# Gate and up projections of a gated FFN as seven block products instead of eight, in a one-core encoder-layer kernel

## The reference

```
def swiglu(x, w_gate, w_up, w_down):
    return (jax.nn.silu(x @ w_gate) * (x @ w_up)) @ w_down
...
D_MODEL = 1024; SEQ = 512; D_FF = 2816
u = rmsnorm(h, ffn1_pre_norm[i])
h = h + 0.5 * rmsnorm(swiglu(u, ffn1_w_gate[i], ffn1_w_up[i], ffn1_w_down[i]), ffn1_post_norm[i])
```

## Time and profile before

| | |
|---|---|
| median of 3 runs | 1209.6 us (1209.51 to 1209.68) |
| span of the profiled execution | 1207.3 us |
| median less span | 2.3 us |
| PE busy | 1198.1 us, 99% |
| PE weight loads busy | 972.3 us, 81% |
| DVE busy | 642.7 us, 53% |
| ACT busy | 466.0 us, 39% |
| POOL busy | 110.2 us, 9% |
| instructions | 15098 |

### The profile page before, as it was taken

One profiled execution on the slowest core, in us unless ns is written; L12 is line 12 of the kernel. 1 busy time (PEld: TensorE's weight loads), 2 busy tenths in 40 slices (PEclk: granted clock), 3 DMA queues, 4 the chain that ended last, 5 costly groups with the idle time before them and its releaser, 6 DMA issues.

```text
span 1207.3 us, 15098 instructions
## 1 busy us (share of the span) xinstructions
PE 1198.1 (99%) x5564; PEld 972.3 (81%) x5564; DVE 642.7 (53%) x1019; ACT 466.0 (39%) x703; POOL 110.2 (9%) x95
## 2 busy tenths in 40 slices
PE   9999999999999999999999999999999999999998
PEld 8888888888888886567887888788888888888887
DVE  6644444462227797755567874674344444222584
ACT  6322333222125537566333623552223232121473
POOL 3000000000004100000012201210000000000254
PEclk9999999999999999999999999999999999999998
DMA  6333232322231341111522233332332323232211
GB/s 224 118 104 103 89 104 87 104 89 103 95 90 53 71 122 53 36 36 36 158 87 71 84 108 105 105 105 87 104 100 91 104 87 105 88 104 92 100 36 70
DMA packets 101840, 111.85 MB, mean 93 GB/s; under 512 B 15294, under 2 KB 91678, under 8 KB 101542
## 3 DMA queue, kind: packets, MB, share of 16 engines
q1 hardware_dynamic: 97542, 109.18, 29.0%
q10 hardware_dynamic: 4256, 2.12, 0.6%
HBM read 108.12 MB, written 3.16 MB: 92 GB/s over the span
## 4 chain that ended last, share of the span: by engine, by line
PE 92%; DVE 3%; ACT 2%; issue 1%; POOL 0%; ACTq 0%; DVEq 0%; POOLq 0%
PE bank L294 25%; PE bank L296 25%; PE bank L295 25%; PE bank L602 2%; PE bank L596 2%; PE bank L597 2%; PE bank L301 1%; PE bank L303 1%; PE bank L302 1%; PE bank L1062 1%; PE bank L436 1%; PE bank L1041 1%; DVE small L1343 1%; PE bank L1729 1%; PE bank L1172 1%
## 5 line engine op out<-in xcount | busy, mean ns | idle before, releaser
L324 DVE TENSOR_TENSOR w_lo<-w_raw,w_hi 128x1024 fp32r<-128x1024 f32 x193 | 242.5, 1262 | 352.5 <-ACT w_hi L317 350.8
L294 PE MATMUL bank<-v_hi,w_hi 128*128 128x512 f32 x904 | 356.8, 395 | 0.0
L296 PE MATMUL bank<-v_hi,w_lo 128*128 128x512 f32 x904 | 352.3, 390 | 0.0
L295 PE MATMUL bank<-v_lo,w_hi 128*128 128x512 f32 x904 | 351.9, 389 | 0.0
L317 ACT ACTIVATE w_hi<-w_raw 128x1024 fp32r<-128x1024 f32 x193 | 202.3, 1056 | 356.4 <-PE bank L296 352.5
L294 PEld LDWEIGHTS bank<-v_hi,w_hi 128*128 128x128 f32 x904 | 169.7, 188 | 38.2 <-issue 3.5
L296 PEld LDWEIGHTS bank<-v_hi,w_lo 128*128 128x128 f32 x904 | 169.7, 188 | 35.7
L295 PEld LDWEIGHTS bank<-v_lo,w_hi 128*128 128x128 f32 x904 | 169.9, 188 | 34.0
L294 PE MATMUL bank<-prod_hi,w_hi 128*128 (+1 forms) x352 | 137.1, 389 | 0.0
L296 PE MATMUL bank<-prod_hi,w_lo 128*128 (+1 forms) x352 | 136.9, 389 | 0.0
L295 PE MATMUL bank<-prod_lo,w_hi 128*128 (+1 forms) x352 | 136.9, 389 | 0.0
(11 more groups left out here) (274 smaller groups left out, 1342.2 us busy)
## 6 DMA issues: line engine op xcount, KB each, us to landing
w_raw<-in_ffn_w_up SPq DMA_DIRECT2D x44, 512.0 KB, 3.5
w_raw<-in_ffn_w_down SPq DMA_DIRECT2D x44, 512.0 KB, 3.4
w_raw<-in_ffn_w_gate SPq DMA_DIRECT2D x43, 512.0 KB, 3.6
w_raw<-in_w_in SPq DMA_DIRECT2D x32, 512.0 KB, 3.7
w_raw<-in_w_out SPq DMA_DIRECT2D x8, 512.0 KB, 3.3
w_raw<-in_ple_w_gate SPq DMA_DIRECT2D x8, 512.0 KB, 3.3
x_tm<-in_x SPq DMA_DIRECT2D x4, 512.0 KB, 6.6
Mb<-m_rows ACTq DMA_DIRECT2D x8, 256.0 KB, 5.0
```

Source lines behind the costliest of these rows:

```text
L294: nc.tensor.matmul(o, whi, a_hi, start=start, stop=False)
L295: nc.tensor.matmul(o, whi, a_lo, start=False, stop=False)
L296: return nc.tensor.matmul(o, wlo, a_hi, start=False, stop=stop)
L324: nc.vector.tensor_tensor(w_lo[:, s, :], w_raw[:, s, :], w_hi[:, s, :].bitcast(F32), ALU.subtract).then_inc(w_lo_done, 1)
```

## The change

Steps 0 and 1 keep the ordinary product (`LEADS = 2`). In the other nine steps of each FFN the gate and the up product (256 features x 1024 x 512 tokens each) are one "quad" each: the 256 output features, the 1024 input features and the 512 tokens are cut in halves, and seven products of 128 features x 512 x 256 tokens replace the eight, by Strassen's scheme in Winograd's form. A quad has 7 products of 12 matmuls with 256 tokens, so 84 in place of 48 with 512 tokens.

- The sums of token blocks (`T1` to `T4`) are made once in each FFN: GpSimd makes the unsplit input `vraw` from `h` beside the sums of squares, DVE the differences, ACT and DVE split them.
- The sums of weight blocks (`S1` to `S4`, 128x512 each) are made by GpSimd in each quad, four instructions, from the raw chunks in `w_raw` to `wsum` (one buffer). ACT and DVE split them in place of raw chunks: 3.5 chunks of 1024 a quad (`group_hi`, `group_lo`, g = 0 to 3), in place of 2 a quad before.
- Partial results are copied from PSUM by ACT (`r_copy_act`) and added to by DVE (`posts_dve`), four times a quad, in `scratch`.
- The gate is scaled and the product made with one instruction of 1024 columns each (`gate_scale_dve`, `prod_dve`), the silu also; the second multiplication by `r_b` falls away, and the norm behind the FFN takes an epsilon divided accordingly (`epsr`).
- The product is kept unsplit (`prod`) and split during the down product (`phi_act`, `plo_dve`), one tile for each chunk, in four slots of `T_hi` and `T_lo`.
- The loop stays on PE alone; DVE, ACT, SP and POOL are written out.

```diff
+        def block_pe(pe, i, q):
+            b = 4 - 4 * q
...
+            own.wait(pe, "post", 8 * i + (4 * q - 4 + POST0 - 8 * LEADS))
+            own.wait(pe, "lead_out", 4 + 4 * q)
+            weights(0)
+            product(0, 0, P, *v(0, 0), 0, 0, True)
+            weights(1)
+            product(1, 0, 2 * P, *v(1, 0), 1, 0, True)
+            weights(2)
+            own.wait(pe, "t_lo", T1 + 1)
+            product(2, 0, P, *T(T1), 2, 1, True)
+            weights(3)
+            own.wait(pe, "t_lo", T2 + 1)
+            own.wait(pe, "rcopy", 6 * i + (3 * q + 1 - 6 * LEADS))
+            product(3, 0, P, *T(T2), 0, 0, False)
+            own.wait(pe, "t_lo", T4 + 1)
+            product(1, P, 2 * P, *T(T4), 2, 0, False)
+            own.wait(pe, "t_lo", T3 + 1)
+            own.wait(pe, "rcopy", 6 * i + (3 * q + 2 - 6 * LEADS))
+            product(2, 4 * P, P, *T(T3), 0, 0, False)
+            product(3, 4 * P, P, *v(1, 1), 3, 0, True)
...
+        FREED = (1, 5, 6, 7)
+        def group_hi(act, qd, g):
...
+            if g < 2:
+                act.wait_ge(*raw_loaded(qd, g))
+            else:
+                own.wait(act, "s_sum", 4 * qd + 2 * g - 2)
...
+                own.wait(act, "mm", 7 * (qd - 1) + FREED[g])
...
+        def r_copy_act(act, qd, e):
+            if qd >= 2 and e == 0:
+                own.wait(act, "prod_ready", LEADS + qd // 2)
+            own.wait(act, "mm", 7 * qd + (1, 4, 6)[e])
...
             # ACT
+            for qd in range(QUADS):
+                r_copy_act(act, qd, 0)
+                group_hi(act, qd + 1, 0)
+                if qd % 2 == 1:
+                    silu_act(act, LEADS + qd // 2)
+                r_copy_act(act, qd, 1)
+                group_hi(act, qd + 1, 1)
+                r_copy_act(act, qd, 2)
+                group_hi(act, qd + 1, 2)
+                if qd == QUADS - 1:
+                    phi_act(act, 0)
+                group_hi(act, qd + 1, 3)
             # DVE
+            for qd in range(QUADS):
+                posts_dve(dve, qd, 0)
+                group_lo(dve, qd + 1, 0)
+                posts_dve(dve, qd, 1)
+                group_lo(dve, qd + 1, 1)
+                posts_dve(dve, qd, 2)
+                group_lo(dve, qd + 1, 2)
+                if qd == QUADS - 1:
+                    plo_dve(dve, 0)
+                posts_dve(dve, qd, 3)
+                group_lo(dve, qd + 1, 3)
+                if qd % 2 == 0:
+                    gate_scale_dve(dve, LEADS + qd // 2)
+                else:
+                    prod_dve(dve, LEADS + qd // 2)
...
+        def pool_prog(pool):
+            def keep_raw(m):
+                nc.gpsimd.tensor_tensor(vraw[:, m, :], h[:, m, :], pre(m).broadcast_to([P, S]), ALU.mult).then_inc(own["vraw_ready"], 1)
+            h_squares_pool(pool, n, keep_raw)
+            for qd in range(QUADS):
...
+                if qd >= 1:
+                    own.wait(pool, "s_lo", 4 * (qd - 1) + 3)
+                nc.gpsimd.tensor_tensor(S1, A21, A22, ALU.add).then_inc(own["s_sum"], 1)
+                nc.gpsimd.tensor_tensor(S3, A11, A21, ALU.subtract).then_inc(own["s_sum"], 1)
+                if qd >= 1:
+                    own.wait(pool, "s_lo", 4 * (qd - 1) + 4)
+                own.wait(pool, "s_sum", 4 * qd + 1)
+                nc.gpsimd.tensor_tensor(S2, S1, A11, ALU.subtract).then_inc(own["s_sum"], 1)
+                own.wait(pool, "s_sum", 4 * qd + 3)
+                nc.gpsimd.tensor_tensor(S4, A12, S2, ALU.subtract).then_inc(own["s_sum"], 1)
```

More of the change, by code:

```diff
@@ L577, in h_squares_pool @@
                 nc.gpsimd.tensor_tensor(sqacc[:], sqacc[:], scratch[:, m % 4, :], ALU.add).then_inc(b["h_acc"], 1)
+            if beside is not None and m < 5:
+                beside(m)
+        if beside is not None:
+            for m in range(5, KD):
+                beside(m)
     def lead_pe(pe, n, N, x_tiles=None):
@@ L676, in sp_prog @@
                 after_lead(sp)
-            with sp.Fori(1, NI) as i:
+            for i in range(1, NI):
                 for j in range(4):
-                    sp.wait_ge(w_lo_done, 4 * i + (N + j - RING + 1))
-                    sp_load(sp, i, j)
[L682 to L688, removed]
@@ new lines, in block_pe, with product, weights, v @@
+        def block_pe(pe, i, q):
+            b = 4 - 4 * q
+            def product(g, off, step, a_hi, a_lo, bank, half, start):
+                s = (N + g) % RING
+                for kk in range(4):
+                    c = off + step * kk
+                    whi, wlo = w_hi[:, s, c:c + P], w_lo[:, s, c:c + P]
+                    o = B[b + bank][:, 256 * half:256 * half + 256]
+                    nc.tensor.matmul(o, whi, a_hi(kk), start=(start and kk == 0), stop=False, skip_group_check=True)
+                    nc.tensor.matmul(o, whi, a_lo(kk), start=False, stop=False, skip_group_check=True)
+                    last = nc.tensor.matmul(o, wlo, a_hi(kk), start=False, stop=(kk == 3), skip_group_check=True)
+                last.then_inc(own["mm"], 1)
+            def weights(g):
+                own.wait(pe, "s_lo", 8 * i + (4 * q + g + 1 - 8 * LEADS))
+            def v(half, t):
+                return [lambda kk, v_=v_: v_[:, 4 * half + kk, 256 * t:256 * t + 256] for v_ in (v_hi, v_lo)]
+            def T(x):
+                return [lambda kk, t_=t_: t_[:, x, kk, :] for t_ in (T_hi, T_lo)]
+            own.wait(pe, "post", 8 * i + (4 * q - 4 + POST0 - 8 * LEADS))
[17 more added lines that the diff above has]
+            product(3, 4 * P, P, *v(1, 1), 3, 0, True)
@@ L709, in down @@
+            with pe.Fori(LEADS, NI) as i:
+                for q in range(2):
+                    block_pe(pe, i, q)
             def down(k, j, first=False):
                 pe.wait_ge(w_lo_done, k + (DN + 1))
-                ph = prod_hi[:, k, :] if isinstance(k, int) else prod_hi[:, bass.ds(k, 1), :].rearrange("p a s -> p (a s)")
-                pl = prod_lo[:, k, :] if isinstance(k, int) else prod_lo[:, bass.ds(k, 1), :].rearrange("p a s -> p (a s)")
+                own.wait(pe, "plo", k + 1)
@@ L713, in down @@
                 for m in range(KD):
[L714 to L718, removed]
+                    if first and m in (0, 4):
+                        own.wait(pe, "post", POST0 + 4 * (QUADS - 1 + m // 4))
+                    last = three(B[YBANK[m]][:], wv(DN + j, m * P, (m + 1) * P), split_slot(T_hi, j), split_slot(T_lo, j),
+                                 first, False)
@@ L754, in ups_dve @@
[L754 to L766, removed]
@@ new lines, in phi_act, with plo_dve @@
+        def phi_act(act, k):
+            own.wait(act, "prod_ready", k // 2 + 1)
+            if k < 4:
+                own.wait(act, "mm", 7 * (QUADS - 1) + 3 + k // 2)
+            else:
+                act.wait_ge(w_used, DN + k - 3)
+            nc.scalar.activation(split_slot(T_hi, k), prod[:, k, :], ACT.Copy).then_inc(own["phi"], 1)
+        def plo_dve(dve, k):
+            own.wait(dve, "phi", k + 1)
+            nc.vector.tensor_tensor(split_slot(T_lo, k), prod[:, k, :], split_slot(T_hi, k).bitcast(F32),
+                                    ALU.subtract).then_inc(own["plo"], 1)
@@ L770, in dve_prog @@
+        def dve_prog(dve, between=None, late=None, arena_free=None):
+            if n == 0:
+                dve.sem_inc(own["post"], POST0)
             lead_dve(dve, n, N)
-            gates_dve(dve, 0, True)
+            gate_scale_dve(dve, 0)
+            T_raw_dve(dve, T1)
             lo_upto(dve, N + 6)
[L773 to L780, removed]
+            T_raw_dve(dve, T2)
+            prod_dve(dve, 0)
+            T_raw_dve(dve, T4)
+            T_raw_dve(dve, T3)
+            lo_upto(dve, N + 7)
+            for x in range(4):
+                T_lo_dve(dve, x)
+            group_lo(dve, 0, 0)
+            group_lo(dve, 0, 1)
+            gate_scale_dve(dve, 1)
+            group_lo(dve, 0, 2)
+            group_lo(dve, 0, 3)
+            prod_dve(dve, 1)
+            if arena_free is not None:
+                arena_free(dve)
+            for qd in range(QUADS):
[11 more added lines that the diff above has]
+                    gate_scale_dve(dve, LEADS + qd // 2)
+                else:
+                    prod_dve(dve, LEADS + qd // 2)
+            for k in range(1, 4):
+                plo_dve(dve, k)
```

309 lines of the change are left out of this document (224 added, 85 removed).

## The result

The changed kernel takes 1252.2 us (median of 4 runs, 1248.4 to 1254.6), beside 1209.6 us before (1209.5 to 1210.3): a ratio of 1.0347, 95% interval 1.0328 to 1.0366. It is slower, as forecast, but by 42.6 us in place of 22.6, and the median lies 2 us above the predicted range.

A forecast was written before the change was run, and what follows sets the result against it. PE's matmul stream bounds the kernel before. Per FFN the quads, with DVE and POOL taking turns, add 8.1 us, the down product's turn 2.7, `vraw` 0.5; twice that is +22.6: 1232 us against 1209.6, range 1196 to 1250.

The forecast's parts named there:

- The mechanism: In the quads, DVE instructions with two SBUF inputs and POOL TENSOR_TENSORs exclude each other and, both queued, take turns.
- The chain from A: From A, the end of an odd quad's sixth product, to the next quad's fourth product, starting at A+8.4, undisturbed A+5.5.
- even P4: Fourth product of even quads: PE starts it 2.9 us late, released by ACT's `scratch` copy.
- the rival of 1196 us: DVE keeps the turn, so S3 falls behind `prod` and `gate_scale`; a pair takes 20.9 us; chance 0.15.
- The mean of `group_lo`: Sign in DVE's splits of the quads: mean well above 1.26 us, 1.5 or more.
- three instructions on one resource: In a quad, 4.2 + 1.2 us of DVE and 4.2 to 5.2 of POOL: about 10 of 9.66 us.
- The narrow matmul: PE's matmul of 256 columns in the quads: 0.115 us, between 0.111 and 0.120; a quad 9.66 us.
- odd P6: Sixth product of odd quads: PE starts it 1.2 us late.
- the clock: Rival: the clock falls in PE's 32 waits, up to +54 us, 1286; chance 0.12 together with slow narrow matmul or loop.
- The nine steps: The nine loop steps of each FFN before the change, which the quads replace: 196.2 us.
- The turns: Start of each down product: its first chunk waits for `plo` of tile 0, +2.7 us an FFN.
- The start of the quads: The 8 `vraw` instructions between and behind the squares mostly hide: 0.5 us an FFN, 0 to 1.5.

The follow-up runs named there:

- e5: The change with one wait number altered: POOL's S1 waits for DVE's split of g=3 in place of g=2; 1203.2 us, ratio 0.9949.
- e7: The change plus second buffer for partial results, S1 behind g=3 and earlier first split of the down product; 1183.3 us, in a second run 1183.2.
- e9: As e7, but the last three `vraw` instructions of each boundary wait until DVE has the second root; 1183.5 us, ratio 0.9786.
- e4: The change plus 18 unused matmuls of 256 columns ahead of the fourth product of each even quad; 1244.6 us, ratio 1.0276.
- e3: The change without the third matmul of each weight (low weights by high tokens) in the quads; 1239.9 us, ratio 1.0252.

## Where the prediction held, and the step that failed

**The mechanism held, with its times.** The chain from A ended at A+8.2 (A+8.4 predicted with 1.29 us for a sum). Late at even P4: 2.47 us, 2.9 predicted; the first matmul after a wait adds 0.11. DVE and POOL took turns: the second sum of a quad, S3, waited for one DVE instruction and then ran in all 36 quads (2.26 to 2.29 us each); that DVE would keep the turn, the rival of 1196 us, was not seen. The mean of `group_lo` was 1697 ns (1.5 us or more predicted), `prod` 2173 (2.2). The Trainium skill (GPSIMD Engine Reference, section 1, Specifications) names this contention, without a figure. The runs give one: a wait for one instruction of the other engine.

**Not quite as said.** I put the loss to three instructions on one resource, "about 10 of 9.66 us, before any ordering". `e5` and `e7` do not bear that out as a bound. `e5` has the same instructions on the same engines, and the later start of the sums alone brings a pair from 23.38 to 20.95 us; with the second buffer too (`e7`) they fit under 10.08 us a quad.

**Terms that were mis-sized.**
- The narrow matmul, taken at 0.115 us between 0.111 and 0.120, is 0.120: the undisturbed first quad has 10.07 us for 84. The 0.0133 us above a cycle per column are thus a fixed cost of each matmul. By itself that is 18 x 0.42 = 7.6 us more an FFN. Behind the longer products more of the chain is hidden, and odd P6 was 0.55 us late, not 1.2: 4.7 us less. That a pair came to 23.38, so near to 23.1, is two errors that cancel in part. Quads without the clock's part: 2 x 10.07 + 8 x 23.38 = 207.2, 11.0 above the nine steps where 8.1 were forecast. Both FFNs: +5.8 us.
- The nine steps, taken at 196.2 us, are 195.8: +0.7.
- The turns: 2.3 us each, not 2.7: -0.9.
- The start of the quads, with its bounds 0 to 1.5: 1.0 and not 0.5 each, +1.1. The squares did not hide `vraw`: as `e9` shows, it held up small DVE instructions on the way to the scale.

**The step that failed is the clock.** It was listed as a rival of its own and set at nothing in the sum, because "the waits here are short and stand between dense products". They were enough, sometimes. In the profiled run the clock fell to half (1.2 GHz) at the end of an even P4's wait, at 178.0 us, for 3.4 us, in which matmuls of 256 columns stood 0.21 us apart:

```profile
178.37 0.58 PE L780 MATMUL bank<-T_hi,w_hi 128*128 128x256 f32 x1 [2.31 <-ACT scratch L1043]
178.75 0.41 PE L781 MATMUL bank<-T_lo,w_hi 128*128 128x256 f32 x1
178.97 0.41 PE L782 MATMUL bank<-T_hi,w_lo 128*128 128x256 f32 x1
179.18 0.41 PE L780 MATMUL bank<-T_hi,w_hi 128*128 128x256 f32 x1
```

Five quads of 36 had such a stretch (85.8, 178.0, 249.7, 915.3, 987.0 us) and took 14.0 to 14.15 us where their like took 12.65. Four of the stretches began in the last 0.4 us of the wait, one 1.4 us behind it. In all, 210.51 + 210.16 - 2 x 207.2 = 6.3 us in the quads, and the 3.2 us in and behind the first down product: +9.5 us. Of the 3.2, half is at 393 us and may be chance: the kernel before has 3.4 us at the low clock at that place, the change 6.8, the second run of `e7` none. Without the 9.5 the run would have taken about 1239 us, inside the forecast's 1219 to 1247. The forecast gave the turns and the clock a chance each, as separate cases; both happened at once, the clock because of the waits. `e4` removes the stretches in the quads and gains 7.6 us, though its filler costs some 5; `e3`, with waits of 4.1 us, has a stretch of 6.8 us in nearly every pair. The runs after that were not profiled had a mean clock of 0.980 to 0.985 against 0.986, and were 3 to 6 us longer: more such stretches would account for that, though no trace was taken of them.

**The sum.** 22.6 + 5.8 + 0.7 - 0.9 + 1.1 + 9.5 = 38.8 of the 39.3 us between the profiled spans; 0.5 us, scattered over the rest, is not explained. Left open too is why 5 of 15 like waits brought the clock down and 10 did not (the sixteenth, one pair behind a low stretch, was only 1.41 us).

## What to carry to other kernels

Before work is moved to POOL because it is idle, lay its instructions beside DVE's two-input ones in time: where both are queued, each pays the other's length, and what decides is whether a buffer that PE waits for hangs behind such a meeting. A wait that lets POOL start later, beside DVE's reads of PSUM, a second buffer and an earlier first split turned 1252 into 1183 us. And where a forecast leaves PE waiting some us again and again amid dense work, charge for the clock as well, by waits that fall and not only as a separate case.

## What the runs showed of the hardware

- A matmul of this format costs 0.120 us at 256 columns and 0.227 at 512: one cycle of 2.4 GHz per column and 13 ns each.
- A DVE TENSOR_SCALAR of four columns, SBUF to SBUF, took 0.82 and 0.97 us beside running POOL TENSOR_TENSORs (`e7`, below), and 0.17 us without them (`e9`): it is not only the two-input ones that wait.

```profile
26.76 5.01 POOL L1094 TENSOR_TENSOR vraw<-h,cols 128x512 f32<-128x512 f32 x3
```

- Additions out of PSUM kept their time beside the same POOL sums. In the timeline of the change, beside the third sum (153.40 to 155.66):

```profile
154.97 0.42 DVE L967 TENSOR_TENSOR scratch<-scratch,bank 128x256 f32<-128x256 f32 x1 [0.45 <-ACT scratch L1043]
```

- Of 15 waits of 2.3 us, some 23 us apart amid work at full clock, five were followed or ended by 3.4 us at the low clock; with matmuls in these waits (`e4`) none was.
